# Three more places for expert weights in two stages, the residual taken from the tokens, and tables loaded later

## The reference, cut to what matters

```python
x = layer_norm(ALPHA * x + att, ln1_g[layer], ln1_b[layer])
h = x.reshape(B * S, D)
expert, gate = route(h, w_router, b_router)
ffn = moe_ffn(h, expert, gate, w_gate[layer], w_up[layer], w_down[layer]).reshape(B, S, D)
x = layer_norm(ALPHA * x + ffn, ln2_g[layer], ln2_b[layer])
```

## Time and profile before

| | |
|---|---|
| Median of 3 runs | 1879.2 us (1876.65 to 1881.16) |
| The profiled execution | 1880.92 us; its span 1879.2 us |
| TensorE busy | 1744.7 us, 93% of the span |
| VectorE, ScalarE, GpSimd busy | 300.7, 266.4, 61.2 us |
| Moved by DMA | 599.91 MB, mean 319 GB/s |
| Chain that ended last | PE 47%, DMA 30%, issue 20% |

### The profile page before, as it was taken

How to read it: one execution, slowest core, us unless ns; L and a number is a source line. 1 busy time by engine, 2 the same in 40 slices (tenths; PEclk the granted TensorE clock), 3 DMA queues, 4 the chain that set the end, 5 groups by cost and what they waited for, 6 DMA issues and landing times.

```text
span 1879.2 us, 18932 instructions
## 1 busy us (share of the span) xinstructions
PE 1744.7 (93%) x8302; PEld 868.5 (46%) x8302; DVE 300.7 (16%) x775; ACT 266.4 (14%) x517; POOL 61.2 (3%) x91
## 2 busy tenths in 40 slices
PE   8999998888988899999898898899999999799997
PEld 7664333332332676433333333256644544655553
DVE  1431000000000334110000000031214031310101
ACT  2301100000000122100000000032230110111111
POOL 3010000000000003010000000000000000000000
PEclk9999999999999899999999999999999999799999
DMA  9748999999999625999999999982424423399993
GB/s 330 261 151 350 428 428 428 428 427 427 427 427 413 235 112 154 352 427 427 428 429 427 428 426 429 416 312 90 177 92 146 167 90 134 146 412 419 418 416 138
DMA packets 89057, 599.91 MB, mean 319 GB/s; under 512 B 5680, under 2 KB 14608, under 8 KB 51840
## 3 DMA queue, kind: packets, MB, share of 16 engines
q1 hardware_dynamic: 84800, 586.28, 76.6%
q0 software_dynamic: 4160, 12.25, 2.2%
HBM read 597.46 MB, written 1.05 MB: 318 GB/s over the span
## 4 chain that ended last, share of the span: by engine, by line
PE 47%; DMA 30%; issue 20%; DVE 2%; ACT 0%; POOL 0%; SPq 0%; POOLq 0%; DVEq 0%
DMA ring<-in_w_up_dram 26%; PE psum L389 23%; PE psum L542 16%; DMA ring<-in_w_down_dram 4%; PE psum L530 1%; PE psum L442 1%; PE psum L576 1%; PE psum L455 1%; PE psum L470 1%; PE psum L384 1%; DMA ring<-in_w_mem_k_dram 0%; PE psum L512 0%; PE psum L938 0%; PE psum L441 0%; PE psum L585 0%
## 5 line engine op out<-in xcount | busy, mean ns | idle before, releaser
L542 PE MATMUL psum<-ring,xT 128*64 128x512 f32 (+1 forms) x3072 | 585.7, 529 | 34.0 <-DMA ring<-in_w_up_dram 23.7
L542 PEld LDWEIGHTS psum<-ring,xT 128*64 128x64 f32 x3072 | 212.0, 137 | 356.6 <-issue 276.4
L542 PE MATMUL psum<-ring,work 128*64 128x512 f32 x1280 | 290.5, 598 | 43.9 <-DMA ring<-in_w_down_dram 42.7
L389 PE MATMUL psum<-ring,xT 128*128 128x512 f32 (+1 forms) x656 | 274.6, 576 | 5.5 <-DVE xT L1593 3.3
L542 PEld LDWEIGHTS psum<-ring,work 128*64 128x64 f32 x1280 | 92.3, 137 | 229.5 <-issue 180.9
L1535 DVE TENSOR_TENSOR work<-work,psum 128x512 f32<-128x512 f32 (+1 forms) x48 | 43.7, 910 | 924.0 <-PE psum L542 924.0
L389 PEld LDWEIGHTS psum<-ring,xT 128*128 128x128 f32 x656 | 123.7, 191 | 143.0 <-issue 134.5
L389 PE MATMUL psum<-xT,ring 128*128 128x256 f32 x544 | 122.0, 384 | 2.2 <-DVE xT L1255 1.5
L389 PEld LDWEIGHTS psum<-xT,ring 128*128 128x128 f32 x544 | 103.4, 192 | 17.4 <-DVE xT L1255 3.0
L530 PEld LDWEIGHTS psum<-work,x 128*128 128x128 f32 x768 | 93.2, 199 | 36.1 <-issue 36.1
L389 PE MATMUL psum<-ring,work 128*128 128x512 f32 (+1 forms) x272 | 106.6, 549 | 1.3 <-DVE work L1255 0.7
(11 more groups left out here) (196 smaller groups left out, 784.5 us busy)
## 6 DMA issues: line engine op xcount, KB each, us to landing
ring<-in_w_gate_dram SPq DMA_DIRECT2D x64, 2048.0 KB, 24.5
ring<-in_w_up_dram SPq DMA_DIRECT2D x64, 2048.0 KB, 23.1
ring<-in_w_down_dram SPq DMA_DIRECT2D x62, 2048.0 KB, 25.6
ring<-in_w_in_dram SPq DMA_DIRECT2D x16, 2048.0 KB, 8.9
ring<-in_w_exp_gate_dram SPq DMA_DIRECT2D x16, 2048.0 KB, 10.4
ring<-in_w_exp_up_dram SPq DMA_DIRECT2D x16, 2048.0 KB, 9.6
ring<-in_w_exp_down_dram SPq DMA_DIRECT2D x15, 2048.0 KB, 12.1
ring<-in_w_in_a_dram SPq DMA_DIRECT2D x3, 2048.0 KB, 24.9
```

Of the source, the lines that this page charges most:

```text
L389: ins = pe.matmul(b[:, cols_at[0]:cols_at[1]], lhsT=lhsT(c), rhs=rhs(c), start=(c == 0), stop=(c == k - 1))
L542: ins = pe.matmul(to[half * CAP:(half + 1) * CAP, 0:n], lhsT=lhsT, rhs=w[:, half * n:(half + 1) * n], start=first, stop=last)
```

## The change

Stages 0 and 1 get three more places of 2 MB for expert pieces, in the working area from float 3328 to its end (`W_MORE_RING`, `MORE_RING`). `Pass` now gives each piece a place: a fixed order of nine in which the new places join (`joining`: before the fourth ring place twice and before the sixth in stage 0; before the fifth twice and before the sixth in stage 1), then always the one whose last use is the oldest; from piece 40 (`AHEAD`) on only the ring. SP waits for the first use of each new place on conditions in `clear`.

To make room, `acc` is no longer written in stages 0 and 1: `keep` multiplies `x` itself by `ALPHA` times the identity, a new constant of 128 columns. `memT` and the keys of the second memory move into `mkv` and `prm`, other buffers move within `work`. On POOL, `dist` goes behind the norm that ends stage 0's expert layer, the parameters of that norm are loaded earlier; the `na_rpb` transfers, `later` and the mask go from stage 1's first norm to behind the mixing norm in stage 2.

```diff
+W_MORE_RING = 3328
+MORE_RING = 3
+AHEAD = 40
...
+    c[:, C_ALPHA:C_ALPHA + P] = ALPHA * np.eye(P)
...
+        memT2 = mkv[:].rearrange("p l k (c t) -> p (l k c) t", t=T)
+        mk2 = prm[:, 0, 1, :].rearrange("p (c t) -> p c t", t=T)
...
+                order = []
+                for k in range(RING + 1):
+                    order += [RING + m for m, at in enumerate(joining) if at == k]
+                    order += [(n0 + k) % RING] if k < RING else []
+                latest = {place: k - len(order) for k, place in enumerate(order)}
+                self.place, self.last, self.landed, uses = [], [], [], {m: sum(o.uses.get(m, 0) for o in before) for m in order}
+                for i in range(self.pieces):
+                    place = min((m for m in order if m < RING or i < AHEAD), key=latest.get)
+                    self.last.append(latest[place])
+                    latest[place] = i
...
-            ph = Pass(wg, wu, wd, width, n_at, slot_main, phases, False)
+            ph = Pass(wg, wu, wd, width, n_at, slot_main, phases, False, {"0": (3, 3, 5), "1": (4, 4, 5), "2": ()}[tag])
...
-                pe.wait_ge(*((S("kept"), 2 * TC * (k + 1)) if k < DEPTH else (S("z_v"), 12)))
                 acc = W(MOE["acc"], TC, 2, 512)
                 for t in range(TC):
                     for half in range(2):
-                        ins = pe.matmul(psum[2 * t + half], lhsT=ident, rhs=acc[:, t, half, :], start=False, stop=last)
+                        if k < DEPTH:
+                            by_rows = x[:, t, half * 512:(half + 1) * 512].rearrange("p (j n) -> p n j", j=ROWS)
+                            ins = pe.matmul(psum[2 * t + half].rearrange("p (n j) -> p n j", j=ROWS), lhsT=alpha_ident, rhs=by_rows, start=False, stop=last)
+                        else:
+                            ins = pe.matmul(psum[2 * t + half], lhsT=ident, rhs=acc[:, t, half, :], start=False, stop=last)
...
-                    if ph in phases[:DEPTH]:
-                        for c in range(TC):
-                            for half in range(2):
-                                cs = slice(half * 512, (half + 1) * 512)
-                                dve.tensor_scalar(in_order(acc[:, c, cs], ROWS), by_rows(x[:, c, cs], ROWS), ALPHA, None, ALU.mult).then_inc(S("kept"), 1)
...
             root("gv")
+            load(2)
             root("ln1_0")
-            pool.wait_ge(S("norm"), NORM_AT["ln1_0"])
+            root("ln2_0")
             pool.dma_start(W(L1["dist"], 3 * TC * T), a["dist"]).then_inc(S("dist_in"), 16)
-            load(2)
             load(3)
-            root("ln2_0")
             load(4)
...
             pool.dma_start(W(W_MEM2, TC, D), a["mem_2"][0].rearrange("(c p) n -> p c n", p=P)).then_inc(S("mem2_in"), 16)
-            pool.dma_start(W(W_AB, W_N - W_AB), a["later"]).then_inc(S("later_in"), 16)
             root("mem")
             root("ln1_1")
-
-            pool.wait_ge(S("norm"), NORM_AT["ln1_1"])
+            load(5)
+            load(6)
+
+            root("ln2_1")
+            root("mix")
...
+            mixed = [(S("mix"), N_SG // 2), (S("att_o"), att_0.out(2))]
+            attended = [(S("att_o"), att_d.out(2))]
+            clear = {(0, 0): mixed, (0, 1): mixed, (0, 2): [(S("norm"), NORM_AT["ln1_0"])],
+                     (1, 0): attended, (1, 1): attended, (1, 2): [(S("norm"), NORM_AT["ln1_1"]), (S("memT_a"), 6)]}
...
-                    if i >= RAW:
-                        sp.wait_ge(sem("used"), plus(i - RAW + 1, B["used"]))
-                    elif not ph.more and ph.n0 + i >= RING:
-                        sp.wait_ge(*freed[ph.n0 + i - RING])
+                    if ph.last[i] >= 0:
+                        sp.wait_ge(sem("used"), plus(ph.last[i] + 1, B["used"]))
+                    elif ph.place[i] >= RING:
+                        for cleared in clear[phases.index(ph), ph.place[i] - RING]:
+                            sp.wait_ge(*cleared)
+                    elif not ph.more:
+                        sp.wait_ge(*freed[ph.n0 + ph.on_ring.index(i) - RING])
```

## The result

| | before | after |
|---|---|---|
| Median of 9 runs | 1881.16 us (1876.65 to 1883.91) | 1870.16 us (1865.70 to 1873.44) |
| Ratio | | 0.994, 95% interval 0.9926 to 0.9954 |
| The profiled execution | 1880.92 us, span 1879.2 | 1871.03 us, span 1869.2 |

The change makes the kernel faster, by 11.0 us in the medians. The forecast was 20.0 us, and 1859.2 us for the time. About half of the gain was right, and most of the difference lies in one step.

What follows compares the result with a forecast made beforehand. The expert layers of stages 0 and 1 were taken as bound by transfers after about three experts. Earlier pieces gave 29.4 us off, `mem_2` 9.4 on, so 20.0 off: 1859.2 us, range 1849 to 1869.

Steps and rivals of the forecast that it cites:

- Part 1: Expert layers of stages 0 and 1: three more places land later pieces 14.7 us sooner in each, 29.4 us off.
- Part 2: Residual by TensorE after the last piece: `keep` reading tokens 512 bytes apart costs 0, with 0 to 7.3 us in the range.
- rival B: Strided `keep` in both expert layers takes twice as long: 7.3 us more, 1866.5 us; chance 0.15.
- Part 3: Distance table, norm parameters and bias tables loaded at other times: cost 0, bias tables ready with a 53 us margin.
- Part 4: Seam before stage 1's expert layer: `mem_2` shares the DMAs with two pieces, 8.4 us later plus 1 for the clock, 9.4.
- the clock: TensorE's granted clock after a pause of some 6 us at the `mem_2` seam: 1 us added.
- A: At the seam `mem_2` keeps its speed, or nearly: 0 to 2.5 us instead of 9.4, 1850 to 1852; chance 0.17.
- C: Strided `keep` matmuls take four times as long or more: 21.8 us more in all, 1881, slower; chance 0.05.
- D: Reloads held up in SP's queue, or TensorE can't keep 25.60 us per expert: half the gain or less, 1869 to 1879; chance 0.11.

## Why the prediction was right in part and wrong in part

**Part 1, three more places: right.** 29.4 us were forecast, 28.7 came (14.5 and 14.2). The mechanism showed at each point named: pieces at 93 us, the first wait at expert 6, experts 29.34 us apart after it.

**Part 2, `keep`: the step that failed.** The working found the place right (after the last piece, paid in full, twice) and the bounds right (0 to 7.3); it then chose 0, "as VectorE's row shows no collapse". 7.0 us came, near the upper bound: 7.14 us for each `keep` instead of 3.63, and 3.63 again as soon as the reading is side by side. This was the mechanism of rival B, at its size. The choice went by a row of another engine: the earlier trace rows has 1.4 ns for each element on VectorE, read at the same step, but the same line gave no row of VectorE reading side by side to compare with, and a matmul wants an element each 0.9 ns, which is faster than anything L1530 could vouch for. It was no bound either: the strided matmul takes 1.7 ns for each element (7.14 us / 8 / 512), more than VectorE's 1.4. The rule of the Trainium skill that stood in the text spoke against the edit, and the trace of after agrees with it. When one bound is backed by a rule about just this pattern and the other by a row of an engine at a lower rate, the value should have been the upper one; the sum would have been 1866.5.

**Part 3, tables moved: right.** 0 was taken and 0 came. From the first issue to the end of the additions it took 33 us where 29 were estimated, and the margin is 51 us (53 forecast). The head of stage 1, where the distance table now loads, gave up 0.5 us, for which no run shows a cause.

**Part 4, `mem_2`: right in mechanism, too small by 1.3 us.** The turns are one for one, as read from the earlier trace rows. From the attention's outputs to ScalarE the delay grew by 9.8 us (720.68 less 721.12 less the lead of -10.22) where 8.4 stood in the sum; the clock took the remaining 0.9, where 1 stood. The missed term is the start: bytes were assumed 1.3 us after the issue, as on idle DMAs, and came after 4.2. In return the transfer itself was shorter than the 12.3 us of the sum: it landed 11.0 us after its first packet.

**The sum.** Put right, it is 28.7 off, 7.0 and 10.7 on, and 0.8 on in smaller parts of the ledger, which makes the 10.2 us of lead at the start of stage 2; the medians differ by 11.0. The range ended at 1869, and the median is 1870.16. Of what it lies above the forecast, 2 us come from the base: the three runs of before had a median of 1879.2, nine have 1881.16. Even the upper bounds of both unknown costs (7.3 for `keep`, 10.4 instead of 9.4 for the seam) only give 1867.5, and 1869.5 with the 2 us of the base; the seam came 0.3 over its bound.

**The rivals.** A fell: `mem_2` did not keep its speed. B came true as a mechanism. C fell: the doubling is the same from 16 bytes up, and doesn't grow with the step. D fell in its reasons: SP's waits held nothing up, and TensorE followed at full lead; a time in its range came about for other reasons, which is why the ledger matters more than the total.

## What to carry to other kernels

Free room for transfers was worth nearly its bytes where the stream was transfer-bound (14.5 and 14.2 us of 14.7), but each transfer that starts earlier takes turns with whatever small one is on the path at that moment; put the small one ahead on the same queue, or issue the large ones on its landing. Let TensorE's moving operand take two float32 elements from each 16 bytes or read side by side, and give a step that can't be avoided to the side that writes PSUM. Work that only adds into an accumulator belongs ahead of a wait for a transfer, never behind the last one.

## What the runs showed of the hardware that I had not expected

- A float32 matmul of 128x512 takes 0.43 us per instruction with its moving operand side by side, 0.45 at a step of 8 bytes, and 0.88 at 16 and 128 bytes (0.89 at 512). Writing the accumulator at steps from 8 to 512 bytes takes 0.43 us each time.
- A transfer issued by POOL while SP's queue is full of 16 KB packets has its first packet 4.2 to 4.3 us after the issue, with packets of 4 KB and of 8 KB alike, against 1.3 us on idle DMAs.
- Between the two queues turns go by packets, 23 to 23 in a microsecond, with four times the bytes for the one with 16 KB packets; on SP's one queue, 1 MB with 4 MB right behind it is in use 4.85 us after its issue.
- The same 123 matmuls between the transposes and the expert layer take 22.1 us of TensorE at a granted clock of 0.93, 23.7 at 0.86 and 24.7 at 0.83. The 0.83 came behind two pauses of 4.82 and 5.16 us; 0.86 and 0.93 both came behind short ones (2.46 and 2.40 us; 2.25 and 1.60), so which of the two a kernel gets the pause ahead of the transposes doesn't settle.
